# Stick-breaking attention: output projection cut into quarters between the head pairs, one mask matmul for both diagonal blocks, VectorE alone splits the output

## The reference

```python
def _stick_breaking(h, w_in, w_out):              # h: (1, 256, 1024); 16 heads of 64, blocks of 128
    q, k, v = to_heads(jnp.split(h @ w_in, 3, axis=-1))
    for each query block i:
        for each key block j from i down to 0:
            z = q_i @ k_j.T / 8
            mask = key position < query position
            log1m = where(mask, log_sigmoid(-z), 0)
            excl = reverse_cumsum(log1m) - log1m
            a = where(mask, exp(log_sigmoid(z) + excl + suffix), 0)
            acc = acc + a @ v_j
            suffix = suffix + sum(log1m)
    return o @ w_out                              # (256, 1024) @ (1024, 1024)
x = x + _stick_breaking(_rmsnorm(x, sb_norm), ...)
x = x + _conv_ffn(_rmsnorm(x, ffn_norm), ...)
```

## Time and profile before

| what | value |
|---|---|
| median of three runs | 1420.74 us (1419.85 to 1421.76) |
| profiled execution | 1420.4 us, span 1418.6 us |
| TensorE | busy 1359.9 us, 96% of the span |
| VectorE, ScalarE | 67%, 47% |
| chain that ended last | PE 89%, DVE 5%, ACT 2% |
| mean granted TensorE clock | 0.987 of full speed |

### The profile page before, as it was taken

One profiled execution on the slowest core, in us unless ns is written; L12 is line 12 of the kernel. 1 busy time (PEld: TensorE's weight loads), 2 busy tenths in 40 slices (PEclk: granted clock), 3 DMA queues, 4 the chain that ended last, 5 costly groups with the idle time before them and its releaser, 6 DMA issues.

```text
span 1418.6 us, 20062 instructions
## 1 busy us (share of the span) xinstructions
PE 1359.9 (96%) x8392; PEld 1195.2 (84%) x8392; DVE 953.3 (67%) x1197; ACT 673.7 (47%) x882; POOL 78.4 (6%) x148
## 2 busy tenths in 40 slices
PE   6999899999998899999899999999999999999997
PEld 1797799998787689998698878999998987999996
DVE  4797787776696776655785445687677534687674
ACT  2543364443546464444444354554455457654542
POOL 1111011110010100000000010000000000000000
PEclk9899999999999899999999999999999999999999
DMA  9787278886493237655355435364553541454530
GB/s 368 275 348 260 89 285 310 296 295 240 136 382 147 90 134 256 223 199 192 110 213 201 155 145 178 131 225 179 181 187 138 210 147 44 159 214 178 184 144 30
DMA packets 46105, 279.41 MB, mean 197 GB/s; under 512 B 5200, under 2 KB 5200, under 8 KB 18880
## 3 DMA queue, kind: packets, MB, share of 16 engines
q1 hardware_dynamic: 33264, 231.57, 44.7%
q0 software_dynamic: 12752, 46.57, 8.7%
HBM read 277.07 MB, written 1.05 MB: 196 GB/s over the span
## 4 chain that ended last, share of the span: by engine, by line
PE 89%; DVE 5%; ACT 2%; issue 1%; DMA 1%; POOL 0%; SPq 0%; POOLq 0%; ACTq 0%; DVEq 0%
PE ps L1634 36%; PE ps L1760 11%; PE ps L1761 11%; PE ps L1762 11%; PE ps L1696 4%; PE ps L1666 3%; PE ps L1727 1%; PE ps L1822 1%; PE ps L1795 1%; DMA ada<-in_ada_w 1%; DVE h_lo L1066 1%; PE ps L2162 1%; DVE x L1098 1%; DVE xn L1096 1%; PE ps L1679 1%
## 5 line engine op out<-in xcount | busy, mean ns | idle before, releaser
L998 DVE TENSOR_TENSOR w_lo<-raw,w_hi 128x2048 fp32r<-128x2048 f32 x210 | 479.7, 2289 | 190.1 <-ACT w_hi L607 189.4
L607 ACT ACTIVATE w_hi<-raw 128x2048 fp32r<-128x2048 f32 x210 | 400.5, 1911 | 218.2 <-PE ps L1634 168.8
L1760 PE MATMUL ps<-h_hi,w_hi 128*128 128x256 f32 x1344 | 383.0, 285 | 1.9 <-ACT m_r L784 1.9
L1761 PE MATMUL ps<-h_lo,w_hi 128*128 128x256 f32 x1344 | 381.5, 284 | 0.0
L1762 PE MATMUL ps<-h_hi,w_lo 128*128 128x256 f32 x1344 | 381.5, 284 | 0.0
L1760 PEld LDWEIGHTS ps<-h_hi,w_hi 128*128 128x128 f32 x1344 | 257.4, 192 | 4.1 <-ACT m_r L784 2.3
L1761 PEld LDWEIGHTS ps<-h_lo,w_hi 128*128 128x128 f32 x1344 | 257.5, 192 | 1.8 <-issue 0.2
L1762 PEld LDWEIGHTS ps<-h_hi,w_lo 128*128 128x128 f32 x1344 | 257.5, 192 | 0.0
L1545 DVE SCALAR_TENSOR_TENSOR f_cv<-ps,cols,f_cv 128x254 f32<-128x254 f32 (+1 forms) x176 | 76.8, 478 | 71.2 <-ACT f_cv L907 69.6
L1634 PE MATMUL ps<-w_hi,h_hi 128*128 128x512 f32 x360 | 120.7, 399 | 0.0
L1634 PE MATMUL ps<-w_lo,h_hi 128*128 128x512 f32 x360 | 118.1, 391 | 0.0
(11 more groups left out here) (286 smaller groups left out, 1652.9 us busy)
## 6 DMA issues: line engine op xcount, KB each, us to landing
raw<-in_stream SPq DMA_DIRECT2D x210, 1024.0 KB, 4.8
ada<-in_ada_w POOLq DMA_DIRECT2D x80, 512.0 KB, 6.3
ada<-in_ada_w SPq DMA_DIRECT2D x8, 512.0 KB, 12.5
raw<-in_ada_w SPq DMA_DIRECT2D x8, 512.0 KB, 15.5
row<-in_gate_b POOLq DMA_DIRECT2D x3, 512.0 KB, 3.9
x<-in_x SPq DMA_DIRECT2D x1, 1024.0 KB, 9.6
retc<-in_retc POOLq DMA_DIRECT2D x1, 1024.0 KB, 5.0
out<-xn SPq DMA_DIRECT2D x2, 512.0 KB, 2.7
```

The costliest lines, as they stand in the source:

```text
L607: act.activation(w_hi[:, s, :], raw[:, s, :], ACT.Copy).then_inc(hi_done[s], 1)
L998: dve.tensor_tensor(w_lo[:, s, :], raw[:, s, :], w_hi[:, s, :].bitcast(f32), ALU.subtract)\
L1760: pe.matmul(out, wh, h_hi[:, kt, :], start=kt == 0, stop=False)
L1761: pe.matmul(out, wh, h_lo[:, kt, :], start=False, stop=False)
```

## The change

Five edits, all in this stage.

1. The score blocks lie in PSUM in another order, with the two diagonal ones side by side, so that one identity matmul of 256 columns for each head takes the place of two of 128. The products with the earlier key block now read and write two pieces of 128 columns with a gap (`earlier_key`). ScalarE makes one more 128x128 copy of the mask near the start of the kernel.
2. All outputs use bank 1. `s_output(p)` waits until the output before it has been split.
3. ScalarE no longer copies the output. VectorE makes both `h_hi` and `h_lo` (`s_split`).
4. The output projection runs in single quarters of six matmuls (`s_project(i, t, n)`). Bank 0 gets chunk 0 after pair 3 and chunk 1 after pair 5; after the last pair come chunks 2 and 3 of bank 0, then bank 1, then banks 2 and 3 in turn.
5. The splits of the weight chunks `C_SO+2`, `C_F1` and `C_F1+1` have new places on ScalarE and VectorE, and the seam is written out.

```diff
-            act.activation(maskr[:, P:4 * P], shp[:, S_CAUS:S_CAUS + 3 * P], ACT.Copy).then_inc(mask_done, 1)
+            act.activation(maskr[:, P:4 * P], shp[:, S_CAUS:S_CAUS + 3 * P], ACT.Copy)
+            act.activation(maskr[:, 4 * P:5 * P], shp[:, S_SBM:S_SBM + P], ACT.Copy).then_inc(mask_done, 1)
...
-                if p >= 1:
-                    s_out(p - 1)
                 if p + 2 < SH_ // 2:
                     s_log(p + 2)
-            s_out(SH_ // 2 - 1)
-            hi(C_SV + 6)
+                if p == 6:
+                    hi(C_SV + 6)
             hi(C_SV + 7)
+            square(X_SB, 0)
+            square(X_SB, 1)
             hi(C_F1)
             hi(C_F1 + 1)
-            boundary(7, X_SB, TR_N7, ...)
+            norm_tile(TR_N7, 0, scale_col, None)
+            square(X_SB, 2)
+            square(X_SB, 3)
...
-                    s_lo(p - 1)
-            s_lo(SH_ // 2 - 1)
+                    s_split(p - 1)
             lo(C_SV + 6)
+            s_split(SH_ // 2 - 1)
             lo(C_SV + 7)
-            for c in range(C_SO, C_SO + 2):
-                lo(c + 4)
-            boundary(add_plain, Y_SOUT, 7, TR_N7, C_F1)
+            add_plain(Y_SOUT, 0)
+            add_plain(Y_SOUT, 1)
+            norm_mean(7, 0)
+            scale_tile(7, 0)
+            lo(C_F1)
+            split_tile(TR_N7, 0, 0, 4)
+            add_plain(Y_SOUT, 2)
+            add_plain(Y_SOUT, 3)
+            norm_mean(7, 1)
+            scale_tile(7, 1)
+            lo(C_F1 + 1)
+            split_tile(TR_N7, 1, 0, 4)
+            lo(C_F1 + 2)
+            lo(C_F1 + 3)
...
-                    for first in (0, T):
-                        last = pe.matmul(ps[:, b, first:first + P], maskr[:, 0:P], maskr[:, 3 * P:4 * P], ...)
+                    last = pe.matmul(ps[:, b, 0:2 * P], maskr[:, 0:P], maskr[:, 3 * P:5 * P], ...)
...
-                if p >= 2:
-                    pe.wait_ge(so_lo, p - 1)
+                if p:
+                    pe.wait_ge(so_lo, p)
...
+                if p in (3, 5):
+                    s_project((p - 3) // 2, 0, 0)
+            s_project(2, 0, 0)
+            s_project(3, 0, 0)
+            for i in range(4):
+                s_project(i, 0, 1)
+            for i in range(4):
+                s_project(i, 1, 0)
+                s_project(i, 1, 1)
+                if i == 2:
+                    norm_tile(7, 0)
             ffn(1, C_F1, TR_N7)
```

More of the change, by code:

```diff
@@ L158, in build @@
         csil = sb("csil", [P, KT])
-        maskr = sb("maskr", [P, 4 * P], f32r)
+        maskr = sb("maskr", [P, 5 * P], f32r)
         gng = sb("gng", [P, GDV])
@@ L412, in ssq_before @@
             return 4 * k if k <= 4 else 4 * k + 4
-        def so_bank(p):
-            return p - 2 if p >= 6 else p % 2
         def early_slot(s):
@@ L956, in s_exp @@
                     .then_inc(sexp, 1)
-            def s_out(p):
-                act.wait_ge(so_mm, p + 1)
-                act.activation(h_hi[:, p, :], ps[:, so_bank(p), 0:T], ACT.Copy).then_inc(so_hi, 1)
             s_log(0)
@@ L967, in _ @@
                 s_exp(p)
-                if p >= 1:
-                    s_out(p - 1)
                 if p + 2 < SH_ // 2:
                     s_log(p + 2)
-            s_out(SH_ // 2 - 1)
-            hi(C_SV + 6)
+                if p == 6:
+                    hi(C_SV + 6)
             hi(C_SV + 7)
+            scale_col = lambda kt: cols[:, COL_FFN + KT + kt:COL_FFN + KT + kt + 1]
+            square(X_SB, 0)
+            square(X_SB, 1)
             hi(C_F1)
             hi(C_F1 + 1)
-            boundary(7, X_SB, TR_N7, lambda kt: cols[:, COL_FFN + KT + kt:COL_FFN + KT + kt + 1], None, C_F1, 5)
+            norm_tile(TR_N7, 0, scale_col, None)
+            square(X_SB, 2)
+            square(X_SB, 3)
+            hi(C_F1 + 2)
+            evacuate(5, 0, (fc_mm, 11), ACT.Copy)
+            norm_tile(TR_N7, 1, scale_col, None)
+            evacuate(5, 1, (fc_mm, 12), ACT.Copy)
+            hi(C_F1 + 3)
+            evacuate(5, 2, multiplied(C_F1), ACT.Copy)
+            evacuate(5, 3, multiplied(C_F1 + 1), ACT.Copy)
             ffn(1, C_F1)
@@ L1584, in s_soft, with s_split @@
                                          s_b[:, p % 3, 0, :, :], ALU.max, ALU.add).then_inc(spm, 1)
-            def s_lo(p):
+            def s_split(p):
+                dve.wait_ge(so_mm, p + 1)
+                dve.tensor_copy(h_hi[:, p, :], ps[:, 1, 0:T]).then_inc(so_hi, 1)
                 dve.wait_ge(so_hi, p + 1)
-                dve.tensor_tensor(h_lo[:, p, :], ps[:, so_bank(p), 0:T], h_hi[:, p, :].bitcast(f32), ALU.subtract)\
+                dve.tensor_tensor(h_lo[:, p, :], ps[:, 1, 0:T], h_hi[:, p, :].bitcast(f32), ALU.subtract)\
                     .then_inc(so_lo, 1)
@@ L2137, in _, with earlier_key @@
                 h_rows(C_SV + i, i, 4)
+            def earlier_key(a):
+                return a.rearrange("p (j c) -> p j c", j=3)[:, 0:3:2, :]
             def s_scores(p):
@@ L2145, in s_scores @@
                 for f, b in half:
-                    pe.matmul(ps[:, b, 0:T], s_k[f, p, 0:P], s_q[f, p, :], start=True, stop=True)
+                    pe.matmul(earlier_key(ps[:, b, 0:3 * P]), s_k[f, p, 0:P],
+                              s_q[f, p, :].rearrange("p (j c) -> p j c", j=2), start=True, stop=True)
                 for f, b in half:
-                    pe.matmul(ps[:, b, T:T + P], s_k[f, p, P:T], s_q[f, p, P:T], start=False, stop=True,
+                    pe.matmul(ps[:, b, P:2 * P], s_k[f, p, P:T], s_q[f, p, P:T], start=False, stop=True,
                               skip_group_check=True)
                 for f, b in half:
-                    for first in (0, T):
-                        last = pe.matmul(ps[:, b, first:first + P], maskr[:, 0:P], maskr[:, 3 * P:4 * P],
-                                         start=False, stop=True, skip_group_check=True)
+                    last = pe.matmul(ps[:, b, 0:2 * P], maskr[:, 0:P], maskr[:, 3 * P:5 * P], start=False, stop=True,
+                                     skip_group_check=True)
                 last.then_inc(z_ready, 1)
@@ L2163, in s_weights @@
                               skip_group_check=True)
-                    last = pe.matmul(ps[:, b, P:2 * P], shp[:, S_NO:S_NO + P], sums[:, 2 * P:3 * P], start=False,
+                    last = pe.matmul(ps[:, b, 2 * P:3 * P], shp[:, S_NO:S_NO + P], sums[:, P:2 * P], start=False,
                                      stop=True, skip_group_check=True)
@@ L2170, in s_output, with s_project @@
                 pe.wait_ge(sexp, p + 1)
-                if p >= 2:
-                    pe.wait_ge(so_lo, p - 1)
+                if p:
+                    pe.wait_ge(so_lo, p)
                 half = [(slice(i * SDH, (i + 1) * SDH), 2 * p + i, s_b[:, p % 3, 0, i, :]) for i in range(2)]
                 for f, h, a in half:
-                    pe.matmul(ps[f, so_bank(p), 0:T], s_v[:, 0, h * SDH:(h + 1) * SDH], a[:, 0:T], start=True, stop=False)
+                    pe.matmul(ps[f, 1, 0:T].rearrange("p (j c) -> p j c", j=2), s_v[:, 0, h * SDH:(h + 1) * SDH],
+                              earlier_key(a), start=True, stop=False)
                 for f, h, a in half:
-                    last = pe.matmul(ps[f, so_bank(p), P:T], s_v[:, 1, h * SDH:(h + 1) * SDH], a[:, T:T + P],
+                    last = pe.matmul(ps[f, 1, P:T], s_v[:, 1, h * SDH:(h + 1) * SDH], a[:, P:2 * P],
                                      start=False, stop=True)
                 last.then_inc(so_mm, 1)
+            def s_project(i, t, n):
+                s = chunk_ready(C_SO + i) if t == n == 0 else (C_SO + i) % NSLOT
+                if t == n == 0:
+                    pe.wait_ge(so_lo, 2 * i + 2)
+                if i == 0 and (t, n) == (0, 1):
+                    pe.wait_ge(so_lo, 8)
+                for k in range(2):
+                    high, low = h_pair(2 * (i // 2))(i % 2, k, t)
+                    for p in range(3):
+                        w = (w_hi, w_lo, w_hi)[p][:, s, k * D + n * 512:k * D + (n + 1) * 512]
+                        last = pe.matmul(ps[:, 2 * t + n, :], (high, high, low)[p], w, start=i == k == p == 0,
+                                         stop=i == 3 and k == 1 and p == 2)
+                if t == n == 1:
+                    last.then_inc(used[s], 1)
+                elif i == 3:
+                    last.then_inc(y_part, 1)
             pe.wait_ge(c_act, 8)
```

## The result

| | median us | lowest to highest of six runs | ratio to before, 95% interval |
|---|---|---|---|
| before | 1421.07 | 1419.85 to 1422.38 | |
| changed | 1430.77 | 1428.99 to 1433.64 | 1.0068 [1.0056, 1.0079] |

The change makes the kernel slower by 0.7%. (Before is a median of six runs here, of three where 1420.74 was given.) The forecast was 1430.5, with 1426.8 to 1433.2 as its range. The profiled execution of the changed kernel took 1431.15 us, its span 1429.4.

The account below looks back on a forecast made before the run. TensorE, almost always busy, was taken to bound the kernel. Profiled 1420.4 + 7.55 (later MLP start) + 2.3 (slow clock) = 1430.25; the median lies 0.3 above the profiled run: 1430.5, range 1426.8 to 1433.2 us.

Parts of the forecast that it names:

- The seam: Projection to MLP: the low part of `C_F1+1` queues on VectorE behind add and scale; 6.5 us new TensorE idle.
- The clock: Behind the idle ahead of the MLP: granted clock falls to 0.50 for about 5 us, costing 2.3 us.
- Rival A: Gap ahead of the MLP: no fall of the clock there; 1428.3 us, chance 0.24.
- one row at 43 us: Profile row where TensorE worked at 1.2 GHz for 5.00 us from 43 to 48, though busy; that loses 2.5 us.
- The chunks C_SO+2 and C_SO+3: Behind the last pair: TensorE waits 2.3 and 1.8 us for their low parts, 4.1 us against a gain of 2.9.
- The masks: In each pair: two 256-column identity matmuls at 0.12 us replace four taking 0.50; 0.26 us saved a pair, 2.1 in eight.
- the forecast's own formula: Pair period: the chain from scores to weights, 3.91 us, and TensorE's work, 3.77, share two periods, so 3.84 each.
- Output on one bank: In the pairs: `s_output` waits for the previous output's split, 0.88 us with signals, covered with 1 us to spare.
- C: Rival: low part of `C_F1+1` in time, only the projection's 1.2 us lost; 1421.9 us, chance 0.03.
- D: Rival: all low parts in time, neither wait forms, 2.9 us gain stays; 1417.8 us, chance 0.03.
- B: Rival: clock also falls in the two waits at 1196 to 1201, 2.3 us more; 1432.8 us, chance 0.13.

Follow-up runs that it names:

- e2: Kernel before, with only the low part of `C_F1+1` moved behind the scale of tile 1 on VectorE: 1427.80 us, ratio to before 1.0049.
- e1: Changed kernel, with the low part of `C_F1+1` moved right behind that of `C_F1` on VectorE: 1422.49 us, ratio to before 1.0013.
- e3: Changed kernel, with 24 spare 512-column matmuls on TensorE between projection and MLP, result unused: 1428.39 us, ratio to before 1.0053.
- e5_quarters: Changed kernel, with three quarters of banks 1 and 2 moved into the waits around the last outputs: 1427.54 us, ratio to before 1.0044.
- e6: Changed kernel, with the low part of `C_F1+1` right behind that of `C_F1` and three quarters moved into the waits: 1419.34 us, ratio to before 0.9985.
- e4: Kernel before, with only the new score layout and one 256-column mask matmul for each head: 1420.20 us, ratio to before 0.9995.

## Why the prediction was right

Times of the changed kernel are given less 0.95 us, the amount by which its first scores came later (1157.67 against 1156.72), so that they can be laid beside the forecast's.

| step | forecast | measured |
|---|---|---|
| masks, saved for each pair | 0.26 us | 0.15 to 0.16 |
| last weights step starts | 1192.05 | 1192.68 |
| last output starts | 1195.0 | 1196.45 |
| quarter of `C_SO+2` | 1198.1 | 1198.61 |
| quarter of `C_SO+3` | 1201.35 | 1201.60 |
| transposes of tile 0 | 1216.4 | 1216.69 |
| wait at the seam | 6.5 | 6.30 |
| MLP starts | 1226.45 | 1226.76 |
| clock, less the short idle at the MLP's start before (0.12 us in the forecast) | 2.2 | 1.8 |
| sum | +9.85 | +9.80 |

The mechanism was right: the order on VectorE made the long wait at the seam, and the wait brought the slow clock. That the sum agrees to 0.05 us is luck: the MLP started 0.31 us later than forecast, and the clock cost 0.36 us less. The result itself is not that sharp, with runs from 1428.99 to 1433.64 us.

*The seam* was the largest term and right step by step: the two adds, 3 us through square, root and scale, and 2.29 us of low part. e2 shows that this line's place alone brings it, e1 that its return alone takes it away.

*The clock* was right in kind. The matmuls that the fall slowed are seen, and e3 removes it while the MLP still starts at the same time, for the same low part (70.02 us behind the first scores, 70.04 in the changed kernel). The net loss is read from the start of the MLP to ScalarE's fourth copy of its first results (`evacuate`): 15.21 us (1227.71 to 1242.92) against 13.40 before (1218.78 to 1232.18), and as well from the MLP's first matmul to the last: 191.04 against 189.22. Against e3 it is 2.1, since e3 takes 0.3 us less than before (188.90). Rival A, no fall, did not happen in any of the three profiled executions with the long wait. How much the fall costs differs, though the waits are alike:

| kernel | wait at the seam | idle until the clock fell | MLP's first matmul to the last | more than before |
|---|---|---|---|---|
| changed | 6.30 | 4.3 | 191.04 | 1.8 |
| e5_quarters | 6.37 | 3.7 | 190.72 | 1.5 |
| e2_seam_only | 6.38 | 3.1 | 190.46 | 1.2 |

The later the clock fell in these three, the more of the MLP ran at half clock: 3.5 us in e2, 4.1 in e5, 4.8 in the changed kernel. The forecast took its loss from one row at 43 us; what was seen here lies below it in all three. It also read the end of the kernel a little short: the mean of 0.62 from 1413 to 1415 puts the fall at about 1413.5, 5.1 us into the idle and not 4.9.

The runs of the changed kernel spread over 4.7 us, with mean clocks of 0.981 and 0.982 in those of 1431.15 and 1433.64 us and of 0.986 in those of 1428.99 and 1429.45, so the loss to the clock may differ from run to run as well; only the first has a profile.

*The chunks C_SO+2 and C_SO+3* were right in kind, their quarters at 0.5 and 0.3 us from the forecast. Instead of two waits of 2.3 and 1.8 us (4.1) there were three of 1.08, 1.28 and 1.36 (3.7), since a part of the first was spent ahead of the last output. e6 and e5 show their price of three to four microseconds by filling them.

*The masks* were mis-sized, and 0.12 us for an identity matmul was one of the signs of being right that did not come. The forecast took the MLP's pace of 0.12 us for each of the two matmuls, so 0.24; from start to start they take 0.34 where nothing holds them (1175.30 to 1175.64 in e4), and 0.15 us is saved. The pace of a long series was used for a pair of matmuls between others of another kind. With 0.15 in place of 0.26 the forecast's own formula gives (3.91 + 3.88)/2 = 3.90 us a pair, which e4 shows (3.92 and 3.90).

*Output on one bank* was the step that failed as it was put: "The wait is covered with 1 us to spare." A wait of `s_output` for the split was even one of the prediction's signs of being wrong, and it came. The sentence holds for seven outputs. The eighth follows the seventh with no weights step between, and waited 1.08 us. It cost little here, because TensorE would then have waited for the low part of `C_SO+2` anyway, which was queued behind the same split. So the 0.9 us by which the last output lay further behind the last weights step than before (3.77 us against 2.90) were swallowed. The 0.6 us by which the last weights step came late were not: about 0.5 are the masks', 0.1 that of the second quarter in the pairs (1.50 us, 1192.13 to 1193.63, where 1.37 was forecast). They reach VectorE, because the split of output 6 starts when that output ends: 0.5 us late at 1195.43. VectorE's two stretches of low part and split then each took 0.1 to 0.2 us less than forecast, which left 0.25 us at the quarter of `C_SO+3` and 0.3 at the transposes. So two small errors of opposite sign stand behind the good agreement here.

*The rivals.* C and D fell with the order on VectorE. Their conditions were made true afterwards: e1, where the low part of `C_F1+1` comes in time, has 1422.49 us against C's 1421.9, and e6, where no wait is left behind the pairs either, but a new one of 1.2 us ahead of tile 1, 1419.34 against D's 1417.8. B, a fall of the clock in the two earlier waits, did not occur in the changed kernel's profiled run (1.00 in all windows from 1194 to 1212), but it did in that of e1, which has the same waits:

```profile
1196.00:1198.00 2.00, 0.72 (x9) 0.46 (x6) 2.00 (x2) 0.43 (x1) 0.00 (x0) 0.85 0.00 0
1198.00:1200.00 2.00, 2.00 (x5) 1.60 (x6) 1.97 (x3) 0.00 (x0) 0.00 (x0) 0.50 0.58 139
```

The quarter between the waits ran at 0.43 us a matmul. It cost nothing, since TensorE would have waited for the second low part otherwise: the quarter of `C_SO+3` starts 44.87 us behind the first scores (1155.94 to 1200.81), in the changed kernel 44.88. So B can happen, in one of the three profiled executions that have these waits (changed, e1, e3), but its price in the forecast, 2.3 us, was too high for this place.

Still open: how often the clock falls at each place, and what sets the moment of the fall, as each kernel has one profile. Not shown apart are the single bank and ScalarE's new order, which no run has alone.

## What to carry to other kernels

When work is moved on one engine, read what is queued in front of each semaphore that another engine's next stage asks for. Here a 2.29 us step that had been hidden ahead of the seam cost 6.3 us and a slow clock once it stood behind the last add, though its own engine had been busy only 6.02 of the 18 us before (1202 to 1220).

Filling holes with small pieces of later work pays (3.2 us between e1 and e6), if the pieces chosen need only what is long ready; the changed kernel turned first to the two chunks that were made last.

A long wait of TensorE can cost more than its length: with 6.3 to 6.4 us of idle came 3.5 to 4.8 us of work at half clock, which lost 1.2 to 1.8 us.

## What the runs showed of the hardware

The granted clock fell from 1.00 to 0.50 (1.2 GHz) while TensorE idled: in the changed kernel at about 1225.7, idle since 1221.4; in e5 at about 1222.4, idle since 1218.8; and in e2 at about 1220.7, idle since 1217.6. In the changed kernel it came back at about 1232.5, after work without a pause from 1227.7, in e5 at about 1229.3 after work from 1225.2, and in e2 at about 1227.5 after work from 1224.0. In e3, with matmuls in the gap up to 0.84 us before the MLP, it stayed at 1.00. In e1, two waits of 1.1 and 1.3 us with 0.9 us of matmuls between were enough for a fall to 0.50 at about 1197.4, where the same waits left the clock at 1.00 in the changed kernel and in e3. So whether short idle brings a fall differs from execution to execution.

Two identity matmuls of 256 columns between other steps take 0.34 us from start to start, and four of 128 take 0.50, while in a long series each of 256 takes 0.12.

A moving operand in two pieces of 128 columns with a gap ran as fast as one of 256: 0.53 us for the scores against 0.54.
